# Latent attention scaled and turned in block pairs, rotary halves exchanged by transfers, and a weight unit split earlier in the recurrent layer

## The reference

```python
def _rope(x, positions, rot_dim):
    half = rot_dim // 2
    ang = positions[:, :, None, None] * inv_freq
    x1, x2 = xr[..., :half], xr[..., half:]
    rot = concatenate([x1 * cos - x2 * sin, x2 * cos + x1 * sin])
def _mla(h, positions, w_in, q_norm, kv_norm, w_uq, w_ukv, w_o):
    c_q, c_kv, k_rope = split(h @ w_in, [384, 640])
    q = (_rmsnorm(c_q, q_norm) @ w_uq).reshape(B, S, 8, 128 + 64)   # 8 heads
    kv = (_rmsnorm(c_kv, kv_norm) @ w_ukv).reshape(B, S, 8, 128 + 128)
    for s0 in range(0, S, 128):            # block-causal, chunks of 64
        s = (q_nope @ k_nope + rope(q_rope) @ rope(k_rope)) * scale
        p = softmax(where(mask, s, -1e30)); outs.append(p @ v[:, :e])
    return o @ w_o
def _rglru_block(...):
    y = gelu(gate_branch) * associative_scan(a, u)    # 1024 channels
    return y @ w_out
```

## Time and profile before

| | us |
|---|---|
| median of three runs | 2122.86 |
| the profiled execution, its own time | 2122.82 |
| span of the profile | 2121.0 |
| PE busy | 2080.4 (98% of the span) |
| PE weight load busy (beside matmuls) | 1702.9 (80%) |
| DVE busy | 1162.4 (55%) |
| ACT busy | 815.6 (38%) |
| POOL busy | 165.9 (8%) |
| chain of waits: share that is PE | 89% |

### The profile page before, as it was taken

The page is one execution under the profiler, slowest core; times in us unless marked ns, Lnnn a source line. Parts: engine busy times, 40 slices in busy tenths (PEclk is TensorE's granted clock), DMA queues, the critical chain, the costliest instruction groups (busy, mean ns, idle before and its releaser), DMA issues.

```text
span 2121.0 us, 25062 instructions
## 1 busy us (share of the span) xinstructions
PE 2080.4 (98%) x9818; PEld 1702.9 (80%) x9818; DVE 1162.4 (55%) x1368; ACT 815.6 (38%) x1156; POOL 165.9 (8%) x184
## 2 busy tenths in 40 slices
PE   8999999999999999999999999999999999999997
PEld 7778888888877888888877788888887778888886
DVE  6766544443886744344667654444476656444344
ACT  6554322323465423132445432232345544232231
POOL 6001000000200200004100100000320001000000
PEclk9999999999999999999999999999999999999998
DMA  6012332233322232323321233223331123223321
GB/s 184 29 60 70 110 99 93 95 99 100 109 70 90 92 98 99 99 90 100 92 80 51 70 110 99 91 97 100 100 94 32 50 80 100 91 97 99 99 90 40
DMA packets 119280, 188.00 MB, mean 89 GB/s; under 512 B 14880, under 2 KB 34208, under 8 KB 119200
## 3 DMA queue, kind: packets, MB, share of 16 engines
q1 hardware_dynamic: 116784, 185.78, 27.3%
q10 hardware_dynamic: 2416, 1.12, 0.2%
HBM read 184.78 MB, written 2.10 MB: 88 GB/s over the span
## 4 chain that ended last, share of the span: by engine, by line
PE 89%; DVE 6%; ACT 4%; issue 1%; DMA 0%; DVEq 0%; SPq 0%; ACTq 0%
PE psum L533 28%; PE psum L534 28%; PE psum L535 28%; ACT arena L2162 1%; PE psum L839 1%; PE psum L826 1%; DVE w_lo L1223 1%; PE psum L953 1%; DVE arena L1532 1%; PE psum L679 1%; DVE small L1518 1%; PE psum L1070 0%; ACT w_hi L1955 0%; PE psum L1100 0%; ACT arena L2150 0%
## 5 line engine op out<-in xcount | busy, mean ns | idle before, releaser
L1223 DVE TENSOR_TENSOR w_lo<-w_raw,w_hi 128x1024 fp32r<-128x1024 f32 x343 | 424.9, 1245 | 794.8 <-ACT w_hi L1955 794.2
L1955 ACT ACTIVATE w_hi<-w_raw 128x1024 fp32r<-128x1024 f32 x343 | 362.6, 1062 | 964.3 <-PE psum L535 964.3
L533 PE MATMUL psum<-h_hi,w_hi 128*128 128x512 f32 x1384 | 546.8, 395 | 0.0
L535 PE MATMUL psum<-h_hi,w_lo 128*128 128x512 f32 x1384 | 538.8, 389 | 0.0
L534 PE MATMUL psum<-h_lo,w_hi 128*128 128x512 f32 x1384 | 538.7, 389 | 0.0
L533 PE MATMUL psum<-u_hi,w_hi 128*128 128x512 f32 x1320 | 519.8, 394 | 6.2 <-DVE w_lo L1223 3.5
L534 PE MATMUL psum<-u_lo,w_hi 128*128 128x512 f32 x1320 | 514.9, 390 | 0.0
L535 PE MATMUL psum<-u_hi,w_lo 128*128 128x512 f32 x1320 | 514.9, 390 | 0.0
L533 PEld LDWEIGHTS psum<-h_hi,w_hi 128*128 128x128 f32 x1384 | 259.9, 188 | 57.5 <-issue 4.3
L534 PEld LDWEIGHTS psum<-h_lo,w_hi 128*128 128x128 f32 x1384 | 259.9, 188 | 56.9 <-issue 4.1
L535 PEld LDWEIGHTS psum<-h_hi,w_lo 128*128 128x128 f32 x1384 | 259.8, 188 | 54.0
(11 more groups left out here) (246 smaller groups left out, 1408.2 us busy)
## 6 DMA issues: line engine op xcount, KB each, us to landing
w_raw<-in_mlp_w SPq DMA_DIRECT2D x256, 512.0 KB, 3.7
w_raw<-in_mla_w_o SPq DMA_DIRECT2D x16, 512.0 KB, 3.5
w_raw<-in_lru_w_in SPq DMA_DIRECT2D x16, 512.0 KB, 4.3
w_raw<-in_swa_w_in SPq DMA_DIRECT2D x12, 512.0 KB, 3.7
w_raw<-in_mla_w_ukv SPq DMA_DIRECT2D x8, 512.0 KB, 4.0
w_raw<-in_lru_w_out SPq DMA_DIRECT2D x8, 512.0 KB, 3.4
w_raw<-in_swa_w_o SPq DMA_DIRECT2D x8, 512.0 KB, 3.6
w_raw<-in_mla_w_in SPq DMA_DIRECT2D x7, 512.0 KB, 3.8
```

The costliest lines, as they stand in the source:

```text
L533: nc.tensor.matmul(out, stat[0], mov[0], start=start, stop=False, skip_group_check=skip)
L535: return nc.tensor.matmul(out, stat[1], mov[0], start=False, stop=stop, skip_group_check=skip)
L1223: nc.vector.tensor_tensor(w_lo[:, to], w_raw[:, to], exact(w_hi[:, to]), ALU.subtract).then_inc(w_ready, 1)
L1955: nc.scalar.activation(w_hi[:, to], w_raw[:, to], ACT.Copy).then_inc(w_hi_done, 1)
```

## The change

1. The five `swap_rows` matmuls of each attention layer go. In their place POOL issues, for the keys and for each pair of queries, four transfers of 32 rows by 512 tokens (64 KB each) from `k_raw` or `q_raw` into new tiles `k_swapped`, `q_swapped`, each exchange with its own wait for the source. DVE reads these tiles, and PSUM areas 1 and 2 are no longer used for it.
2. `normalised(i)` works in two halves: blocks 3 and 2 once their exponentials are done, then 1 and 0. `transposes(i)` turns the blocks 3 and 2 (seven pieces) after the first half, the other three after the second. `turned(i)` copies area 3 first.
3. The order on DVE and ACT at the start of an attention layer: `latent_scales` before `key_rope`, `keys(0)` before `query_rope(0)`; ACT loads the square-root table, and then the exponential table, by small unused operations ahead of need. PE's sums come right behind `rope_queries(0)`.
4. In later pairs `query_rope(n)` stands behind `normalised`, `query_rope_hi(n)` behind `turned`. One `split(1)` moves from the end of the attention layer to the start of its heads.
5. In the recurrent layer DVE splits the fourth unit of the output product right behind `recurrence(7)`; before it stood behind the last `y_lo`.

```diff
+            def swap_halves(to, rows, swapped):
+                for at in range(0, P, ROPE):
+                    for a, b in ((at, at + 32), (at + 32, at)):
+                        g.dma_start(to[a:a + 32, :], rows[b:b + 32, :]).then_inc(swapped, 16)
...
+                    pool.wait_ge(rows_ready, i + 1)
+                    swap_halves(mla_m["k_swapped"], k_raw, k_swapped)
+                    for pair in range(PAIRS):
+                        pool.wait_ge(area_free[1], jobs["mla", i, "queries area", pair])
+                        swap_halves(mla_m["q_swapped"], q_raw, q_swapped)
...
                 def query_rope(n):
-                    done("swap", n)
-                    nc.vector.tensor_tensor(rope, bank(1, 1), sin[:, :], ALU.mult).then_inc(area_free[1], 1)
+                    dve.wait_ge(q_swapped, 64 * (PAIRS * j + n + 1))
+                    nc.vector.tensor_tensor(rope, mla_m["q_swapped"], sin[:, :], ALU.mult)
...
                 def transposes(i):
+                    def turn(b, tiles):
...
                     c.add("p")
                     pe.wait_ge(p_ready, c.now("p"))
+                    claim(2)
+                    turn(3, (0, 1))
+                    turn(2, (0, 1))
+                    claim(3)
+                    turn(3, (2, 3))
+                    turn(2, (2,)).then_inc(psum_done, 1)
+                    summed("transposes", i, 3)
+                    c.add("p")
+                    pe.wait_ge(p_ready, c.now("p"))
+                    turn(1, (0, 1))
+                    turn(0, (0,)).then_inc(psum_done, 1)
+                    summed("transposes", i, 2)
...
                 query_lo(0)
+                latent_scales()
                 key_rope()
-                latent_scales()
+                key_scales()
+                keys(0)
                 query_rope(0)
                 key_rope_lo()
-                key_scales()
-                keys(0)
                 query_rope_lo(0)
                 key_lo(0)
+                split(1)
                 query_lo(1)
...
                 recurrence(7)
+                split(1)
                 y_lo(2)
                 y(3)
                 y_lo(3)
-                split(5)
+                split(4)
```

More of the change, by code:

```diff
@@ L727, in rope_queries @@
                     claim(1)
+                    jobs["mla", j, "queries area", n] = c.now("area1")
                     for k in range(3):
@@ L731, in rope_queries @@
                     used("rope", n)
[L733 to L745, removed]
                 def latent_sums():
@@ L815, in scores @@
                         summed("scores", i, a)
-                    jobs["mla", j, "scores area", i] = c.now("area3")
+                    jobs["mla", j, "scores areas", i] = c.now("area2"), c.now("area3")
                 def transposes(i):
+                    def turn(b, tiles):
+                        for jt in tiles:
+                            a = 2 + jt // 2
+                            at = T_OFF[jt] + P * (b - jt) - (0 if a == 2 else 896)
+                            mm = nc.tensor.transpose(area(a)[:, at:at + P],
+                                                     mla_m["p"][:, S_OFF[b] + P * jt:S_OFF[b] + P * (jt + 1)], ident)
+                        return mm
                     c.add("p")
                     pe.wait_ge(p_ready, c.now("p"))
[L821 to L829, removed]
+                    claim(2)
[10 more added lines that the diff above has]
+                    summed("transposes", i, 2)
                 def weighted(i):
@@ L893, in mla @@
                 scores(2)
-                swap_queries(2)
                 keys(2)
@@ L1439, in key_rope @@
                 def key_rope():
-                    done("swap keys")
                     dve.wait_ge(area_free[2], jobs["mla", j, "tables area"])
-                    nc.vector.tensor_tensor(rope, bank(2, 1), sin[:, :], ALU.mult).then_inc(area_free[2], 1)
+                    dve.wait_ge(k_swapped, 64 * (j + 1))
+                    nc.vector.tensor_tensor(rope, mla_m["k_swapped"], sin[:, :], ALU.mult)
                     link(nc.vector.tensor_tensor(k_raw, k_raw, cos[:, :], ALU.mult))
@@ L2168, in turned @@
                 def turned(i):
+                    done("transposes", i, 3)
+                    nc.scalar.activation(mla_m["pt"][:, 896:ATT], area(3)[:, 0:384], ACT.Copy).then_inc(area_free[3], 1)
                     done("transposes", i, 2)
                     nc.scalar.activation(mla_m["pt"][:, 0:896], area(2)[:, 0:896], ACT.Copy).then_inc(area_free[2], 1)
-                    done("transposes", i, 3)
-                    nc.scalar.activation(mla_m["pt"][:, 896:ATT], area(3)[:, 0:384], ACT.Copy).then_inc(area_free[3], 1)
                 def out_hi(i):
@@ L2181, in mla @@
                 query_raw(0)
+                link(nc.scalar.activation(unused_roots, ones[:, 0:QB], ACT.Sqrt))
+                latent_roots()
+                link(nc.scalar.activation(unused_roots, ones[:, 0:QB], ACT.Exp))
                 key_rope_hi()
-                latent_roots()
+                key_hi(0)
                 query_rope_hi(0)
-                key_hi(0)
+                split(1)
                 values(0, 2)
```

39 lines of the change are left out of this document (19 added, 20 removed).

## The result

The kernel after takes 2105.39 us (median of 4 runs, 2104.97 to 2105.56), the kernel before beside it 2122.72 us (2122.41 to 2123.12): a ratio of 0.992, 95% interval 0.9908 to 0.9931, 17.3 us less. The profiled execution took 2105.36 us, its span is 2103.6 us, 17.4 less than before's.

A forecast was written before the change was run, and what follows sets the result against it. PE, busy 98% of the span, was taken to bound the kernel. Per attention layer 10.0 us goes and 6.75 comes; two layers give 6.5, the recurrent layer 6.6, so 13.1 us off 2122.8: 2110 us, range 2105 to 2120.

The forecast's parts named there:

- the last rival: Heads 3 and 5 and POOL's exchange: lists lengthen less than counted and the exchange is quick, 2106 us, chance 0.08.
- Recurrent layer: PE's 3.47 us stop for a weight unit's low part and the slow clock behind it go: 6.6 us gained.
- The exchange of pair 1: Head 1 of each attention layer: this exchange is not hidden, giving a new stop of 2.6 us in transposes(1).
- largest(1) at the landing + 7.7: Head 1: largest(1) starts 7.7 us after the exchange lands, through operations on DVE and copies on ACT.
- stop = D - 2.8: Head 1: the stop in transposes(1) is the exchange time D less 2.8 us.
- D: Time from finished source to finished exchange by POOL: taken as 5.4 us, between bounds of 4.2 and 7.6 us.
- The chain of the halves: Head 1: first transpose 4.2 us after largest(1) starts, 1.5 us sooner; the wait for the second half counts as nothing.
- Heads 3 and 5: Stops of 1.2 and 0.85 us stay there, with DVE's list between two heads some 0.5 us longer.
- The opening: Start of an attention layer: key-scale and area 0 stops go, a 1.7 us stop comes at scores(0); gain 1.5 us.
- What goes: Each attention layer loses five swap matmuls, 4.3 us, and stops of 4.15, 0.94 and 0.62 us: 10.0 us.
- The clock: Rival: the clock falls behind a transposes(1) stop as long as 3.47 us, costing 3.1 us a layer; chance 0.16.
- The other rivals: Among them, POOL issues slowly, 2127 us, chance 0.08; POOL stands while DVE works, 2120.5 us, chance 0.04.

The follow-up runs named there:

- lru_only: The kernel before with only the recurrent layer's split moved behind recurrence(7): 2116.24 us, ratio 0.9974.
- rope_first: The kernel after with heads 2 and 4 ordered as before (query_rope ahead of normalised, query_rope_hi ahead of turned): 2102.94 us, ratio 0.9909.
- halves_only: The kernel before with only the new normalised, transposes and turned by block pairs, swap matmuls and orders kept: 2112.38 us, ratio 0.9953.
- whole_heads: The kernel after with normalised, transposes and turned by whole heads again: 2122.30 us, ratio 1.0003.
- pieces2: The kernel after with each of POOL's four transfers of an exchange issued as two of 16 rows: 2111.73 us, ratio 0.9954.
- pieces3: The kernel after with each of POOL's four transfers of an exchange issued as three of 11, 11 and 10 rows: 2120.81 us, ratio 0.9994.

## Why the prediction was right, point by point

It said 2110 us, 2105 to 2120, faster; measured were 2105.4. The direction and the places came out, the size is 4.6 us off, at the very edge of the range and outside the forecast's own 2107 to 2114. What came is the last rival, a quick exchange and shorter lists, 2106 us, which had a chance of 0.08; that the range holds the result, by 0.4 us, is owed to its having been drawn around that case; in the size that is luck. Layer 0 by stretches, as gains in us, predicted and measured between the landmarks above and those of before:

| stretch | predicted | measured |
|---|---|---|
| start of the heads to `scores(0)` | 1.5 | 1.11 |
| to `transposes(1)` | 0.86 + 0.79 - 2.6 = -0.95 | 0.60 |
| to `transposes(3)` | 0.86 + 1.40 - 1.2 - 0.4 = 0.66 | 1.15 |
| to `transposes(5)` | 0.86 + 0.94 - 0.85 = 0.95 | 1.25 |
| to `weighted(7)` | 0.52 + 0.52 = 1.04 | 1.47 |
| sum | 3.2 | 5.58 |

- *Recurrent layer, 6.6 us*: right in mechanism and size (6.65 in the trace; 6.0 us in the time of `lru_only`), and the fifth unit was covered.
- *The exchange of pair 1*: the mis-sized term. The chain "largest(1) at the landing + 7.7" and the rule "stop = D - 2.8" held (1.17 us at a D of 3.9, then 2.69, 4.11 and 4.99 in the runs with more pieces, 0.1 us over the rule each). D itself was 3.9 us, not 5.4, and lay under the lower bound of 4.2: the issue was at that bound (0.49 us), the 0.57 us until the first issue and in the gap behind it were not in it, but the landing took 1.9 us and not 2.7. The bound was not one: the 2.7 us are of loads of `in_positions`, the nearest row there was, while these go from one tile of the core to another. That is 1.4 us in layer 0 and 1.7 in layer 3 (a stop of 0.91), so that PE's longest stop in the layer is `scores(0)` and not `transposes(1)`.
- *The chain of the halves*: `largest(1)` starts at 85.19 in after (DVE's timeline, below this list), the transposes at 89.42, 4.23 us (4.2 predicted). Heads 6 and 7 have no stop, as predicted, and the wait for the second half is nothing.
- *Heads 3 and 5, "1.2 and 0.85 us stay"*: 0.85 and 0.63. That the new order lengthens the list is confirmed in direction by `rope_first`, 0.66 us for 0.5, but against the kernel before nothing was lost: from `largest(2)` to `largest(3)` it takes 13.84 us, before 13.90. The prediction named the cause, `query_rope_hi` behind `turned` on ACT, but left out what pays for it: counted from `largest(2)`, ACT begins `turned(2)` at 6.05 us, where it was 7.01 before, since the transposes come sooner.
- *The opening, "both stops go"*: the stop at the key scales stayed with 0.50 us in layer 0 (0.2 in the other), `scores(0)` waits 1.52 us (1.7 predicted).
- *What goes*: a stop costs PE its listed idle and about 0.2 us more (`halves_only`: 9.9 to 10.5 us for 8.3 listed), which I had not counted. It is most of the excess of the last stretch.
- *The clock*: 1.00 in the attention layers, so this rival did not come about. `whole_heads`, `pieces2` and `pieces3` show that it is real, but it was mispriced: 1.0 to 1.6 us a stop and not 3.1 (in `pieces2` the low clock lasted 3 to 4 us and not 6.4), and from stops as short as 2.08 us and not from 3.47. At my own D of 5.4 it would have been at hand: layer 3 of `pieces2` has that D, a stop of 2.69 us and the low clock.
- *The other rivals*: POOL did not issue slowly, and did not stand while DVE worked: its first issue came 0.3 us behind its release, at 73.87, and the other three, 74.66 to 76.13, ran beside `keys(1)`, the second line here.

```profile
85.19 0.19 DVE L1509 MEMSET psum<- 64x64 f32 x2
...
74.88 1.23 DVE L1490 TENSOR_TENSOR arena<-psum,arena 128x1024 f32<-128x1024 f32 x1 [1.00 <-PE psum L537]
```

On the two rules. The Trainium skill, "DMA: Bandwidth & Descriptors", gives about 1 us until the first byte of a transfer that POOL issues ("Latency and other measured facts"), and its fit in "Anatomy of one DMA" makes an estimated 2.15 us of 64 KB. The prediction took the 1 us for the distance between issues, which the page does not say it is; the trace shows 0.49 us for each further issue. From issue to landing it shows 1.9 us, descriptors included, a little under the estimate, and the measurement decides. The trace agrees with the page in that the fixed cost, not the 64 KB, makes the time: 32 KB took 1.8 us.

The Trainium skill, "SBUF — State Buffer", "SBUF: two separate sides", has POOL unable to write descriptors while DVE runs an operation that takes both ports, as the prediction took the multiplications to be. The only sign in after is the gap of 0.28 us behind the first issue, at 74.37, when DVE had already ended them (at 73.88); `pieces2` has no gap in this place, and one of 0.30 us in its opening, at 52.96, where DVE was idle. No run here puts the two side by side for long enough to show the rule right or wrong.

Where the gain is, is an answer that the prediction did not give: not in the exchange. 6 to 7 us are the recurrent layer's, 10 to 11 the halves', and the exchange with its openings brings 1.3 us at most until the splits are out of its way.

## What to carry to other kernels

Taking work off the busiest engine brings only what the engines behind it can follow: the result that PE had at once now comes by way of another engine's queue, and nearly all of the saved 5.8 us a layer turned into stops. Look for what the waiting engine could do in the meantime: three splits of 1.2 us a layer, made sooner, brought 6.6 us, where the exchange without them had brought 1.3 at most. And where a stop has one releaser, look who comes next behind it before pricing its end: in the opening the second wait ended within a microsecond of the first, and moving only one of them brought nothing.

## What the runs showed of the hardware

- A transfer of 64 KB from tile to tile, issued by POOL, took 0.49 us to issue and 1.9 us from issue to landing; halves (32 KB) took 0.48 and 1.8 us, thirds (20 and 22 KB) 0.51 us to issue and 1.8 and 1.9 to land. Between 20 and 64 KB the number of transfers in a row counts, their bytes hardly.
- A stop of PE costs some 0.2 us over its listed idle time (`halves_only`: ten stops, 8.3 us listed, 9.9 to 10.5 us gained).
- The granted clock fell to 0.50 behind stops of 2.08, 2.31, 2.69, 4.11, 4.27 and 4.99 us and behind a pair of 1.06 us (at 1606.11) and 1.88 us (at 1612.33), and cost 1.0 to 1.6 us behind each of the single ones; the one of 3.47 us in before was followed by it too. It stayed at 1.00 behind others of 2.08, 2.31 and 2.57 us. What tells these from those was not tested.
